# The order of the routed experts in a decoder layer: triples of token counts run outwards from the middle

## The reference, cut to what matters

```python
_, idx = lax.top_k(masked, TOP_K)            # 8 of 64 experts for each token
counts = jax.ops.segment_sum(ones, flat_e)   # tokens of each expert, 8192 in all
hid = jax.nn.silu(xb @ w1[e]) * (xb @ w3[e]) # 1024 -> 256, for the tokens of expert e
ob = (hid @ w2[e]) * rw[:, None]             # 256 -> 1024, weighed by the router
y = y.at[rt].add(ob)                         # added to the rows of these tokens
```

## Time and profile before

| what | value |
|---|---|
| median of 3 runs | 2469.95 us (2466.83 to 2470.83) |
| the profiled execution: own time | 2450.18 us |
| the profiled execution: span | 2448.5 us |
| mean granted TensorE clock | 0.996 |
| PE busy | 97% of the span |
| VectorE, ScalarE, GpSimd busy | 50%, 20%, 27% |
| DMA, whole span | 435.27 MB, 178 GB/s |
| DMA, from 1656 to 2400 us | 298 to 361 GB/s by stretch |

### The profile page before, as it was taken

How to read it: one execution, slowest core, us unless ns; L and a number is a source line. 1 busy time by engine, 2 the same in 40 slices (tenths; PEclk the granted TensorE clock), 3 DMA queues, 4 the chain that set the end, 5 groups by cost and what they waited for, 6 DMA issues and landing times.

```text
span 2448.5 us, 32891 instructions
## 1 busy us (share of the span) xinstructions
PE 2383.8 (97%) x8512; PEld 1164.5 (48%) x8513; DVE 1212.5 (50%) x2776; ACT 487.4 (20%) x900; POOL 655.3 (27%) x652
## 2 busy tenths in 40 slices
PE   5999999999999999999999999999999999999997
PEld 3444444555544555665544545444444444444443
DVE  3376212666754666667468666433333333343332
ACT  4311000444433133333222112200000000000000
POOL 0000000000022100000245144455545545455541
PEclk9999999999999999999999999999999999999998
DMA  8222333443362333212434313589899999999995
GB/s 261 46 73 46 82 78 113 109 140 108 110 183 66 90 77 99 80 54 82 134 114 142 105 57 148 183 293 307 283 302 336 334 325 337 314 367 362 322 319 132
DMA packets 121191, 435.27 MB, mean 178 GB/s; under 512 B 21004, under 2 KB 23260, under 8 KB 95376
## 3 DMA queue, kind: packets, MB, share of 16 engines
q1 hardware_dynamic: 78208, 306.91, 36.1%
q0 software_dynamic: 42896, 127.25, 19.3%
HBM read 366.44 MB, written 71.70 MB: 179 GB/s over the span
## 4 chain that ended last, share of the span: by engine, by line
PE 89%; DVE 6%; DMA 2%; issue 1%; ACT 1%; SPq 1%; POOL 0%; DVEq 0%; POOLq 0%; ACTq 0%
PE psum L1031 22%; PE psum L1552 18%; PE psum L1619 9%; PE psum L1116 8%; PE psum L1557 5%; PE psum L1368 4%; PE psum L1418 3%; PE psum L1362 2%; PE psum L1625 2%; PE psum L1321 2%; PE psum L1462 2%; PE psum L1187 2%; PE psum L1197 2%; PE psum L1206 2%; PE psum L1485 1%
## 5 line engine op out<-in xcount | busy, mean ns | idle before, releaser
L1031 PE MATMUL psum<-mem 128*128 128x512 f32 x1536 | 690.1, 594 | 1.5 <-DMA mem<-in_w_in 1.2
L1552 PE MATMUL psum<-mem 128*128 x1008 | 449.9, 594 | 1.9 <-DVE mem L2851 1.3
L1031 PEld LDWEIGHTS psum<-mem 128*128 128x128 f32 x1536 | 279.2, 191 | 294.3 <-issue 290.5
L836 POOL DMA_INDIRECT mem<-h_d,idx x287 | 294.0, 1024 | 361.1 <-DVE idx L2952 261.9
L1552 PEld LDWEIGHTS psum<-mem 128*128 128x128 f32 x1008 | 186.4, 190 | 230.2 <-issue 230.2
L2930 DVE TENSOR_TENSOR mem<-mem,psum 128x256 f32<-128x256 f32 x93 | 39.2, 421 | 424.4 <-ACT mem L2046 422.9
L1619 PE MATMUL psum<-mem 128*128 128x512 f32 x504 | 227.9, 599 | 1.9 <-issue 1.3
L1116 PE MATMUL psum<-mem 128*128 128x512 f32 x448 | 192.8, 592 | 0.0
L841 POOL DMA_INDIRECT out_x<-mem,put x93 | 140.5, 1511 | 93.8 <-issue 68.5
L1619 PEld LDWEIGHTS psum<-mem 128*128 128x128 f32 x504 | 92.8, 190 | 125.7 <-issue 125.7
L1116 PEld LDWEIGHTS psum<-mem 128*128 128x128 f32 x448 | 84.9, 190 | 105.7 <-issue 105.0
(11 more groups left out here) (449 smaller groups left out, 2681.1 us busy)
## 6 DMA issues: line engine op xcount, KB each, us to landing
mem<-in_exp_w SPq DMA_DIRECT2D x201, 1024.0 KB, 10.8
mem<-in_w_in SPq DMA_DIRECT2D x16, 2048.0 KB, 14.2
proj_d<-mem SPq DMA_DIRECT2D x104, 256.0 KB, 2.0
mem<-in_ada_w POOLq DMA_DIRECT2D x16, 1024.0 KB, 6.2
mem<-proj_d POOLq DMA_DIRECT2D x56, 256.0 KB, 3.4
mem<-proj_d POOLq DMA_DIRECT2D x20, 512.0 KB, 5.4
mem<-in_ada_w SPq DMA_DIRECT2D x4, 2048.0 KB, 23.1
mem<-in_w_branch SPq DMA_DIRECT2D x3, 2048.0 KB, 8.0
```

The costliest lines, as they stand in the source:

```text
L836: g.indirect_dma_start(x[:, 2 * P * n:2 * P * (n + 1)], None, h2_q, bass.IndirectOffsetOnAxis(ap=idx[:, p, j, n:n + 1], axis=0), bounds_ch ...
L1031: mm = t.matmul(bank(unit_bank(u)), l, r, start=(k == 0), stop=(k == KD - 1))
L1552: return t.matmul(bank(up_banks[j][r]), xgT[r][:, k, P * j:P * (j + 1)], up_piece(h, r, k), start=(k == 0), stop=(k == KD - 1))
```

## The change

It rewrites the three instructions that fill `turn_of`:

```diff
             turns, third = turn_of.rearrange("e (k j) -> e k j", j=3), NR // 3
-            v.tensor_copy(turns[:, :, 0:1], col_i[0:NE, 0:third].unsqueeze(2))
-            v.tensor_scalar(turns[:, :, 1:2], col_i[0:NE, 0:third].unsqueeze(2), -1.0, float(NR - 1), ALU.mult, ALU.add)
-            v.tensor_scalar(turns[:, :, 2:3], col_i[0:NE, 0:third].unsqueeze(2), float(third), None, ALU.add)
+            v.tensor_scalar(turns[:, :, 0:1], col_i[0:NE, 0:third].unsqueeze(2), -1.0, float(third - 1), ALU.mult, ALU.add)
+            v.tensor_scalar(turns[:, :, 1:2], col_i[0:NE, 0:third].unsqueeze(2), float(2 * third), None, ALU.add)
+            v.tensor_scalar(turns[:, :, 2:3], col_i[0:NE, 0:third].unsqueeze(2), -1.0, float(2 * third - 1), ALU.mult, ALU.add)
```

## The result

The changed kernel takes 2475.53 us (median of 10 runs, 2471.26 to 2478.13), the kernel before 2469.96 us (10 runs, 2464.77 to 2473.46): a ratio of 1.0029 [1.002, 1.0038]. The forecast was no change at 2470.0 us; the time lies inside its range, but 5.6 us above the forecast, and the interval of the ratio does not contain 1.

A forecast was written before the change was run, and what follows sets the result against it. TensorE (PE) was taken to set the pace, transfers close behind. All terms summed to 0 (ends -1.5 and +3.8 us), giving 2450.2 us for the profiled execution, plus the unplaced 19.8 us: 2470.0 us, range 2464 to 2477.

The forecast's parts named there:

- The turns: Sorted routed experts: the change runs the same twenty triples backwards, with the order within each triple kept.
- the sum of PE's work: Expert stage: the same 57 full and 27 half sorted tiles with the same instructions before and after, 0 us.
- D: Four triples of 3 full and 1 half tiles, the big expert's second tile a half one; period 37.7 us.
- C: Three sorted triples of 2 full and 2 half tiles, the densest in transfers at 361 GB/s; period 33.9 us.
- The transfers: Weight loads in the sorted triples: the reversal keeps the tightest lead, 16.2 us; taken as 0, ends 0 and +3.3 us.
- R1: Slower: transfers can't keep up with C in its new, earlier place; +10.9 us, 2480.9 us, chance 0.07.
- R2: Slower: the last two-tile expert's late scatters hold up the tail, at most 7.15 us, 2477.1 us; chance 0.02.
- PE's small idle times: Three PE gaps of 0.33 to 0.36 us inside triples; at best all go, -1.0 us; taken as 0.
- I let it stand as an equal addition: The timed median's 19.8 us above the profiled execution, not located on the page, was added unchanged to the forecast.
- R3: Faster: timed runs have stalls in C that the profile lacks, and the new order removes them; 2459.1 us, chance 0.08.
- The end: Last sorted expert, now two tiles: its scatters keep about 7 us of spare time before the overflow entries' scatters; 0.
- the exit seam: Where the last sorted triple meets the 89-row overflow entry, a new neighbour; taken as 0, 0.5 us either way.

The follow-up runs named there:

- c_before: The kernel before with no edit, run again for a second profile; its expert stage takes 865.4 us, 15.2 us more than in the first profile.
- c_after: The changed kernel with no further edit, run again for a second profile; its expert stage takes 877.8 us, 12.4 us longer than that of c_before.
- e_dcab: Against the kernel before, triples reordered to old numbers 19 down to 13, then 0 up to 12; ratio 1.0048.
- e_bcda: Against the kernel before, triples reordered to old numbers 4 up to 19, then 0 up to 3; ratio 1.0053.

## Why the prediction was wrong, point by point

- **The turns, the set-up, the sum of PE's work: right.** The reversed triples, the counts and the periods of D and C came out to a tenth of a microsecond.
- **The transfers and R1: right that C's new place costs nothing.** C idles no more there, and half the bytes change the idle time of the stage by some 2 us (18.2 to 16.1 with the old order).
- **R2: right that it is nothing.** From PE's last instruction to the end of the span it is 15.9 us, before 16.5.
- **PE's small idle times: wrong, and this is the step that failed.** I bounded them by the rows of one execution: "At best all three go: -1.0 us", and for a loss no end at all. The same kernel in c_before idles 18.2 us in this stage, mostly in front of the downs, and the changed one 23.9 and 28.3 us in its two profiles.
- **"I let it stand as an equal addition": wrong.** Of the 19.8 us between the median and the profiled execution, 15.2 us (by c_before) were time of the very stage that was changed, and it hangs on how the entries lie against the runs of gathers. What an order changes is just that. R3 named the premise, stalls that the profile lacks, at a chance of 0.08, but put them into C and gave them the wrong sign.
- **The end, "0", and the exit seam, "0.5 either way": wrong by 8.95 us, and it is here that the first error shows.** I looked at the scatters there. What counted was the copy of line 2049 for the last sorted largest expert: with k = 0 last it falls into a half tile of the smallest expert, with 1.6 us of cover, during six gathers and two scatters in a row. The idle time and the clock are 6.72 + 2.23 = 8.95 us. The medians differ by 5.6 us, so some 3 us were won elsewhere; one candidate is an idle time of 3.35 us that c_before has in C, at 2244 us, where the change has none over 0.4. With single profiles that sum can't be closed: by c_before and c_after the stages differ by 12.4 us.
- **The range held the time by luck.** It was widened towards R1 to R3, none of which happened.

Shown by runs: that the last sorted triple decides (one triple moved, both ways); that the wait there is for a signal of TensorE that comes 7.2 us late; that the difference between the orders goes when the gathers are cut to a third, and the late signals with it; that a swap within the triples removes most late copies; and that the total of the bytes changes little. Argued only: that the steps of 0.7 us and the late signals are one thing, and that it begins in GpSimd's runs of gathers and not in the full DMA engines that go with them.

Open, and a rival that no run tested: the recording itself. The first profiled execution had the same gathers, no late copy and 15,536 records of landings; all other traces lack some of these records (they have 10,329 to 11,370) and show steps, few where the gathers are few. Each timed run comes with the span and the clock of its core, so that it was recorded in some form too, and the runs can't say whether the late signals would be there without the recorder. Open as well: why the idle time is 6 us at the last triple and 1.0 to 1.8 at most other two-tile experts, though runs of gathers are there too; whether number, bytes or rate of the gathers matters; and why e_dcab and e_bcda are some 5 us above the change.

## What to carry over

Before bounding a change by a profile, set the profiled execution's own time against the median: here they were 19.8 us apart, 3.5 times the effect, and the missing time was of a kind that the change could move. When entries of unequal size are ordered, ask for each product that crosses engines how much work of the consumer stands between, and try a middle entry, not the smallest, behind the largest: here that took 0.42% off the time of before with the reversed order and 0.16% with the old one, though not by the cover that I had in mind.

## What was not expected of the hardware

- Around runs of indirect DMAs on GpSimd, signals between other engines came late, in all profiled executions with the full number of gathers but one: TensorE's transpose ended at 2387.48, its semaphore update is recorded at 2394.69, and ScalarE's copy started at 2394.71, while TensorE itself went on with its next twelve matmuls without a pause. Two neighbouring issues of SP lay 1.43 us apart where they had been 0.44. The bar of such a gather (1.01 us) shows nothing of it. The Trainium skill ("Perfetto Trace Analysis", DMA Instruction — SWDGE (GPSIMD)) says that such a bar ends with the writing of the descriptors and not with the transfer. The bars here can't confirm it; in the 7.5 us of this wait the DMA engines were at 0.98 of their time with 383 GB/s, all queues together.
- Neither the number of steps nor that of late copies sets the difference between the orders: the change has 131 and 13 and c_before 156 and 14, and the change is slower. Where they fall does.
- In the idle time of 6.72 us the clock fell to 1.2 GHz for 6.8 us, 2.3 us before it ended, which added 2.23 us to the 16 matmuls behind it. At one of 3.35 us in c_before it fell for 3.4 us; at those of 1.1 to 1.7 us in the changed kernel it didn't. The length of the idle time doesn't tell it alone: in c_after it fell at one of 2.11 us, in e_dcab it didn't at one of 2.37.
